# A seventh set of expert weights, and the down weights issued from ScalarE's queue

## What is computed

```python
    flat = g_idx[..., None] * EXPERTS_PER_GROUP + ei              # 4 groups x 8 experts, 2 per token
    combine = jnp.sum(jax.nn.one_hot(flat, N_EXPERTS) * (g_w[..., None] * ew)[..., None], axis=-2)
    a = jnp.einsum('bld,edf->blef', h, w_gate)                    # 32 x 1024 x 256
    u = jnp.einsum('bld,edf->blef', h, w_up)                      # 32 x 1024 x 256
    act = jax.nn.silu(a) * u * combine.astype(h.dtype)[..., None]
    return jnp.einsum('blef,efd->bld', act, w_down)               # 32 x 256 x 1024
...
    y_prompt = rmsnorm(yp, norm_final)
```

## Time and profile before

| | |
|---|---|
| median of three runs | 761.89 us |
| the profiled execution | 762.18 us |
| its span, first to last instruction | 760.4 us |
| moved by the transfers | 243.00 MB, mean 320 GB/s |
| busy: TensorE, VectorE, ScalarE, GpSimd | 655.6, 306.8, 142.4, 139.0 us |

### The profile page before, as it was taken

One profiled execution on the slowest core, in us unless ns is written; L12 is line 12 of the kernel. 1 busy time (PEld: TensorE's weight loads), 2 busy tenths in 40 slices (PEclk: granted clock), 3 DMA queues, 4 the chain that ended last, 5 costly groups with the idle time before them and its releaser, 6 DMA issues.

```text
span 760.4 us, 13782 instructions
## 1 busy us (share of the span) xinstructions
PE 655.6 (86%) x5037; PEld 461.6 (61%) x5037; DVE 306.8 (40%) x1552; ACT 142.4 (19%) x406; POOL 139.0 (18%) x209
## 2 busy tenths in 40 slices
PE   5999999998999978999998999927897879667674
PEld 3888888677888856755432877626653445434331
DVE  3004987998868588610000121354324111111103
ACT  3122223233325322120010000120100101101013
POOL 0169964762000223200000000011000000000000
PEclk9999999999999999999999999957999898899997
DMA  9938989889988988977999989366999999999971
GB/s 309 260 127 281 312 271 401 288 279 342 360 292 281 392 273 287 382 275 275 390 409 386 297 320 409 140 256 239 361 394 401 348 382 401 402 400 402 416 285 59
DMA packets 94918, 243.00 MB, mean 320 GB/s; under 512 B 8850, under 2 KB 54546, under 8 KB 86530
## 3 DMA queue, kind: packets, MB, share of 16 engines
q1 hardware_dynamic: 57906, 192.99, 67.7%
q10 hardware_dynamic: 31328, 32.00, 12.7%
q0 software_dynamic: 5616, 17.11, 6.8%
HBM read 235.00 MB, written 9.11 MB: 321 GB/s over the span
## 4 chain that ended last, share of the span: by engine, by line
PE 56%; DMA 25%; DVE 13%; SPq 2%; issue 2%; ACT 1%; ACTq 0%; POOL 0%; DVEq 0%; POOLq 0%
PE zps L913 32%; DVE kall L1402 6%; PE nps L1087 5%; DMA ring_all<-in_w_up 5%; PE nps L1212 4%; DMA kall<-in_w_up 3%; DMA zret<-in_w_up 3%; DMA gain<-v_rows 3%; DMA qb<-in_w_down 3%; DMA ring_all<-in_w_ret_o 3%; PE zps L1235 3%; DMA out<-sfin 2%; PE nps L884 2%; DMA ring_all<-in_w_down 1%; SPq L444 1%
## 5 line engine op out<-in xcount | busy, mean ns | idle before, releaser
L913 PE MATMUL zps<-hT,ring_all 128*128 128x264 f32 x1152 | 274.8, 393 | 1.6 <-DVE hT L1583 1.0
L913 PEld LDWEIGHTS zps<-hT,ring_all 128*128 128x128 f32 x1152 | 217.4, 193 | 45.0 <-issue 5.3
L1402 DVE CUSTOM_DVE_ANT_0 kall<-kall,qb 128x128 f32<-128x128 f32 x512 | 153.0, 364 | 60.0 <-DMA kall<-in_cache_k 56.9
L620 POOL DMA_INDIRECT zatt<-h_rows,tidx_i x16 | 15.0, 939 | 349.4 <-DVEq L1671 194.4
L913 PE MATMUL zps<-headT,ring_all 128*128 128x264 f32 x256 | 58.5, 388 | 3.7 <-DMA ring_all<-in_w_ret_o 2.3
L913 PEld LDWEIGHTS zps<-headT,ring_all 128*128 128x128 f32 x256 | 48.1, 190 | 14.8 <-issue 4.8
L1087 PE MATMUL nps<-ring_all,zret 128*64 128x512 f32 x224 | 51.6, 599 | 2.8 <-DMA ring_all<-in_cache_v 2.8
L1745 DVE TENSOR_TENSOR qdT<-qdT,nps 128x64 f32<-128x64 f32 x32 | 7.1, 221 | 107.5 <-ACT qdT L825 107.0
L669 ACT ACTIVATE zt<-zps 128x264 f32<-128x264 f32 x56 | 21.8, 390 | 149.4 <-PE zps L913 148.0
L1212 PE MATMUL nps<-ring_all,zatt 128*32 128x128 f32 x768 | 30.0, 311 | 13.9 <-DMA ring_all<-in_w_up 12.4
L1570 DVE TENSOR_TENSOR hT<-zps,zatt 128x264 f32<-128x264 f32 x8 | 3.5, 433 | 93.1 <-PE zps L913 92.9
(11 more groups left out here) (364 smaller groups left out, 839.5 us busy)
## 6 DMA issues: line engine op xcount, KB each, us to landing
kall<-in_cache_k SPq DMA_DIRECT2D x64, 512.0 KB, 6.4
ring_all<-in_cache_v SPq DMA_DIRECT2D x56, 512.0 KB, 8.2
ring_all<-in_w_in ACTq DMA_DIRECT2D x26, 1024.0 KB, 8.8
ring_all<-in_w_gate SPq DMA_DIRECT2D x12, 1024.0 KB, 15.6
ring_all<-in_w_up SPq DMA_DIRECT2D x12, 1024.0 KB, 17.6
ring_all<-in_w_down SPq DMA_DIRECT2D x10, 1024.0 KB, 15.7
ring_all<-in_w_in SPq DMA_DIRECT2D x6, 1024.0 KB, 13.6
kall<-in_w_gate SPq DMA_DIRECT2D x5, 1024.0 KB, 22.8
```

The costliest lines, as they stand in the source:

```text
L620: pool.indirect_dma_start(out=rows, out_offset=None, in_=h2_rows, in_offset=bass.IndirectOffsetOnAxis(ap=col, axis=0), bounds_check=T - 1, ...
L913: mm = pe.matmul(zps[m % 2][:, 0:T], w[:, k, P * fb:P * (fb + 1)], rhs[:, k, :], start=(k == 0), stop=(k == KT - 1))
L1402: ins = v.tensor_tensor_reduce(kh, kh, qb[b % 2][:, P * h:P * (h + 1)], 1.0, 0.0, ALU.mult, ALU.add, scores[:, pg, AH * b + h:AH * b + h + 1])
```

## The change

The number of sets goes from 6 to 7. The seventh's gate and up lie in the first 4,096 columns of `zatt`, its down weights in the columns of the constants that only the mixers use. Small tiles share new ones (`rows_a`, `rows_b`) to make room: `h2n`, `xg`, `xgT` and `ysb` leave `zatt`, for `gain`, `rows_a` and `rows_b`. The two gathered tiles now lie on partitions 0 to 63 and 64 to 127 of `rows_b`; `x_tr` turns them with ordinary matmuls placed in the rows of the array where the data are, not with transposes. `xgT` takes the tile `gain`, so the final gain is loaded by SyncE behind the last expert's gate and up product. The down weights from expert 7 on are issued by ScalarE, a quad's four behind `pick_copy`; SyncE's loop has gate and up alone.

```diff
-SETS = 6
+SETS = 7
...
-        lgs = sb("lgs", [G + NE, T])
+        rows_a, rows_b = sb("rows_a", [P, DM]), sb("rows_b", [P, DM])
...
-        xg = [zflat[0:2 * CAP, DM * i:DM * (i + 1)] for i in range(2)]
-        ysb = zflat[:, 2 * DM:3 * DM]
+        xg = [rows_b[2 * CAP * i:2 * CAP * (i + 1), :] for i in range(2)]
+        ysb = rows_a
...
-        gate_up_w.append(headT[:, :, 0:2048])
+        gate_up_w += [headT[:, :, 0:2048], zflat[:, 0:4096].rearrange("p (a c) -> p a c", a=2)]
...
-                  scr[:, 0:2048], qb_all[:, :, :].rearrange("p a b -> p (a b)")]
+                  scr[:, 0:2048], qb_all[:, :, :].rearrange("p a b -> p (a b)"), cst[:, COL["causal"][0]:COL["causal"][0] + 2048]]
...
-        xgT = [zflat[:, 3 * DM + 512 * i:3 * DM + 512 * (i + 1)] for i in range(2)]
+        xgT = [gain[:, 512 * i:512 * (i + 1)] for i in range(2)]
...
-        h2n = zflat[:, 0:3 * DM].rearrange("p (t d) -> p t d", t=3)
+        h2n = (gain, rows_a, rows_b)
...
             down_in(0, 0)
+            gate_up_in(6, 6)
             sp.wait_ge(z_ready, 2 * (N_IN + 2 * N_O))
             gate_up_in(5, 5)
...
             down_in(1, 1)
+            down_in(6, 6)
...
-            def next_down(e):
-                sp.wait_ge(e_D, 2 * ((e - SETS) // 4 + 1))
-                down_in(e % SETS, e)
-
-            downs = SETS
+
             for e in range(SETS, NE):
                 sp.wait_ge(e_GU, e + 1 - SETS)
                 gate_up_in(e % SETS, e)
-                while downs <= min(e - (4 if e < 16 else 2), NE - 5):
-                    next_down(downs)
-                    downs += 1
...
+            sp.wait_ge(e_GU, NE)
+            sp.dma_start(gain[:, :], norm_final.rearrange("(o d) -> o d", o=1).partition_broadcast(P)
+                         .rearrange("p o d -> p (o d)")).then_inc(fgain, 16)
...
+            for lo, hi in ((0, T), (328, 584), (648, DM)):
+                link(pool.memset(rows_b[:, lo:hi], 0.0))
...
-            act.dma_start(gain[:, :], norm_final.rearrange("(o d) -> o d", o=1).partition_broadcast(P)
-                          .rearrange("p o d -> p (o d)")).then_inc(fgain, 16)
-
...
+            def next_downs(q):
+
+                act.wait_ge(e_D, 2 * (q + 1))
+                for e in range(4 * q + SETS, min(4 * q + SETS + 4, NE)):
+                    if e < NE - 4:
+                        down_in(e)
+                    else:
+                        down_half(e, 0, d_in[e % SETS])
+                if 4 * q + SETS + 4 >= NE:
+                    for e in range(NE - 4, NE):
+                        down_half(e, 1, d_last)
...
                 if e % 4 == 2:
                     pick_copy(e // 4, P, e // 4 + 1)
+                if e % 4 == 2 and e >= 6 and 4 * (e // 4 - 1) + SETS < NE:
+                    next_downs(e // 4 - 1)
...
                 for k in range(KT):
-                    mm = pe.transpose(zps[0][:, 2 * CAP * k:2 * CAP * k + rows], xg[par][0:rows, k:DM:KT], ident[0:rows, 0:rows])
+                    at = slice(2 * CAP * par, 2 * CAP * par + rows)
+                    mm = pe.matmul(zps[0][:, 2 * CAP * k:2 * CAP * k + rows], xg[par][0:rows, k:DM:KT], ident[at, at],
+                                   start=True, stop=True, tile_position=(2 * CAP * par, 0))
```

More of the change, by code:

```diff
@@ L208, in build @@
         zt = [sb(f"zt{i}", [P, T]) for i in range(2)]
+        lgs = zt[0][0:G + NE, :]
         qb_all = sb("qb", [P, 2, DM])
@@ L212, in build @@
         scores = sb("scores", [P, NPG, NB * AH])
-        vnT = sb("vnT", [P, NB * AH])
+        vnT = rows_b[:, 584:584 + NB * AH]
         sn8 = sb("sn8", [NB, AH])
-        rtmp = sb("rtmp", [P, 2, 2, P])
-        rtmd = sb("rtmd", [32 + NB, 1, 2, P])
+        rtmp = rows_a[:, 0:512].rearrange("p (a b c) -> p a b c", a=2, b=2)
+        rtmd = rows_b[0:32 + NB, 328:584].rearrange("p (a b c) -> p a b c", a=1, b=2)
         scr = sb("scr", [P, 2304])
@@ L224, in build @@
         qdT = sb("qdT", [P, P])
-        s1 = sb("s1", [P, RDV])
-        sfin = sb("sfin", [P, RDV])
-        qkd = sb("qkd", [P, 2, RH * NB])
+        s1, sfin = rows_a[:, 512:768], rows_a[:, 768:1024]
+        qkd = rows_b[:, 264:328].rearrange("p (a b) -> p a b", a=2)
         ptab = sb("ptab", [1, NB * NPG], I32)
@@ L350, in build @@
             "y_square", "t_oh", "t_pos", "t_lhs", "t_idx", "t_e2"))
-        t_x, t_exp, t_tabs = map(sem, (
-            "t_x", "t_exp", "t_tabs"))
+        t_exp, t_tabs = map(sem, (
+            "t_exp", "t_tabs"))
         x_in2 = [sem(f"xg_in{i}") for i in range(2)]
@@ L362, in build @@
         fgain = sem("fgain")
-        h2_scaled = sem("h2_scaled")
         block = ctx.enter_context(nc.Block())
@@ L484, in _ @@
                 gate_up_in(e % SETS, e)
-                while downs <= min(e - (4 if e < 16 else 2), NE - 5):
-                    next_down(downs)
-                    downs += 1
[L488 to L492, removed]
-                    sp.dma_start(down_w[e % SETS].rearrange("p (f n) -> p f n", f=FB)[:, :, 512 * half:512 * (half + 1)],
-                                 w_down[0, bass.ds(e, 1), :, 512 * half:512 * (half + 1)].rearrange("o (f p) n -> p (o f) n", p=P)
-                                 ).then_inc(signals[e % SETS] if signals else d_last, 16)
             sp.wait_ge(t_exp, 1)
@@ L622, in gather @@
                                         bounds_check=T - 1, oob_is_err=False).then_inc(x_in2[par], 16)
-            def gather_for(p):
+            for p in range(NPAIR):
                 if p >= 2:
@@ L627, in gather_for @@
                 gather(p % 2, xg[p % 2], tidx_i[0:2 * CAP, p:p + 1])
-            for p in range(2):
-                gather_for(p)
-            for p in range(2, NPAIR):
-                gather_for(p)
             base = link_n[0]
@@ L794, in _ @@
                 copy(xT[:, k, :], zps[k % 2][:, 0:T]).then_inc(x_Tc, 1)
+            act.wait_ge(r_st, 16 * RH)
             act.wait_ge(v_used, N_V)
@@ L835, in y_copy, with down_in, down_half @@
                 copy(ysb[rows, 512 * half:512 * (half + 1)], bank[rows, :]).then_inc(e_Dc, 1)
+            def down_in(e):
+                act.dma_start(down_w[e % SETS].rearrange("p (f n) -> p f n", f=FB),
+                              w_down[0, bass.ds(e, 1)].rearrange("o (f p) n -> p (o f) n", p=P)).then_inc(d_in[e % SETS], 16)
+            def down_half(e, half, signal):
+                act.dma_start(down_w[e % SETS].rearrange("p (f n) -> p f n", f=FB)[:, :, 512 * half:512 * (half + 1)],
+                              w_down[0, bass.ds(e, 1), :, 512 * half:512 * (half + 1)].rearrange("o (f p) n -> p (o f) n", p=P)
+                              ).then_inc(signal, 16)
+            def next_downs(q):
[8 more added lines that the diff above has]
+                        down_half(e, 1, d_last)
             def pick_copy(q, rows, n):
@@ L1182, in tile_base @@
             def tile_base():
-                pe.wait_ge(t_x, 1)
+                pe.wait_ge(t_lhs, 3)
                 pe.matmul(mps[:, 640:640 + NE], xcnt_b, upper[0:NE, 0:NE], start=True, stop=True)
@@ L1187, in tile_rows @@
             def tile_rows():
-                pe.wait_ge(t_lhs, 3)
+                pe.wait_ge(t_lhs, 4)
                 row_table(bps[:, 768:768 + XT], xA, xB)
@@ L1694, in tile_counts @@
                 link(v.tensor_copy(xcnt_b, xcnt.to_broadcast([NE, P])))
-                v.sem_inc(t_x, 1)
+                v.sem_inc(t_lhs, 1)
             def tile_tables():
```

8 lines of the change are left out of this document (4 added, 4 removed).

## The result

The changed kernel takes 780.07 us in the median of four runs (777.95 to 781.06), against 761.5 us for the kernel before beside it: a ratio of 1.023, with a 95% interval of 1.0197 to 1.0264. I had forecast 757.0 us, faster by a little. It is slower by 15 to 20 us by the interval, 18.6 us by the medians. The profiled execution took 779.74 us, its span is 777.9 us.

The account below looks back on a forecast made before the run. Weight transfers, not TensorE, were taken to bound the expert stage. Terms -8.0 - 1.5 + 1.2 + 2.4 + 1.0 = -4.9 us took the median of 761.89 to 757.0 us, range 751 to 765.

Parts of the forecast that it names:

- The 15 other pairs: Matmul turns after the first in the expert stage: 0.6 us more each, hidden in TensorE's slack, so 0.
- The first pair's term (+2.4): First turn behind the router, at half clock: matmuls dearer than transposes and delaying SyncE's next transfer, +2.4 us.
- the first rival: At the turn and the final gain: the turn is no dearer and the gain hides, 753.6 us; chance 0.22.
- The tail: Last experts' weights: the last halves, issued by ScalarE behind `pick_copy`, start later and leave the DMA engines idle, +1.2 us.
- The two terms of ScalarE's queue, -1.5 and +1.2: Moving down weights: -1.5 us for DMA dips at 549 and 606 us removed, +1.2 us for last halves issued later.
- The seventh set's -8.0: Around the router: three transfers leave the saturated expert stage for idle DMA time, -8.0 us.
- the gain's +1.0: Final gain's 512 KB load, moved into the tail beside the last halves, +1.0 us.
- The fourth rival: Expert stage: two queues of weights lower the transfer rate, up to 18 us more, 775 us; chance 0.13.
- the figure of the sum: Expert stage: 396 GB/s as the rate of the full DMA engines, making a 1,024 KB transfer worth 2.65 us.
- The third: Rival at the router: the seventh down transfer delays the first gather by up to 2.65 us, 759.7 us; chance 0.08.
- The fill: Seventh set's early transfers around the router: gate and up fill 475 to 480 us, down weights end about 509.1.
- The second rival: ScalarE's issues block in the expert stage, 2.77 us each, 11 us a quad, giving 760 us; chance 0.12.

Follow-up runs that it names:

- e1: The changed kernel with the gathered rows turned by transposes again, ScalarE's queue and seven sets kept: 761.41 us, ratio 0.9976.
- e3: The changed kernel with each turning matmul loading 128 neighbouring columns instead of every eighth: 766.04 us, ratio 1.0044.
- e8: The changed kernel with the turning matmuls loading every second column instead of every eighth: 766.8 us in its one run.
- e9: The changed kernel with turning matmuls for pairs 0 to 7 only and transposes for 8 to 15: 769.78 us, ratio 1.0103.
- e4: The changed kernel with transposes again and the down weights back in SyncE's queue, seven sets kept: 757.03 us, ratio 0.9894.
- e12: Repeat of e4 (seven sets, transposes, SyncE's queue alone) on another chip: 756.53 us, ratio 0.9946.
- e5: The kernel before with down weights from expert 6 on issued by ScalarE; six sets, transposes, early gain: 767.57 us, ratio 1.0028.
- e6: e1 with each gate and each up transfer cut in two of 4 KB rows: 762.41 us, ratio 0.9976.
- e2: The kernel before with the turn by ordinary matmuls, all on partitions 0 to 63: 790.69 us, ratio 1.0295.

## Why the prediction was wrong

**The step that failed** is "The 15 other pairs add 0.6 us each, 9 us in all, beside 48 us of slack: 0." Each adds 2.9 us, 44 us in all, of 48, and it was not hidden: e1, without them and the first, is 18.7 us faster. The first pair's term (+2.4) was nearly right: measured 2.9 us, and SyncE's first issue stands 519.19 - 510.59 = 8.6 us behind the start of the turn where it stood 5.7 us behind. What was wrong was the row for full clock. I took 0.105 us from line 1122, a matmul whose weights are neighbouring columns; the turn loads every eighth. At half clock my nearest row had the right number for another reason: there the clock sets the pace, and the step hardly shows (0.23 to 0.25 us). At full clock the step does. The rows had a hint: the transposes took 1.11 and 1.09 us at either clock. I read it, in the first rival, as a sign that the turn might be cheap. It said that something other than the array's clock set their pace. For the matmuls e3 and e8 show what: the step; for the transposes no run varies it. For a form with twice the instructions at that step I had no row, and should have kept 4 us as the upper bound for every turn.

The sentence from the Trainium skill that I set beside it ("TensorE: Matmul & The Clock Gate", section "Terms", the transpose mode four times as fast for float32) is nearly what the trace shows for this turn: 4.03 against 1.11 us, 3.6 times. I worked it out for the first pair only. For all sixteen, as an estimate from that page, it would have been 3.3 x 16 = 53 us, over the slack. At a step of 1 the runs don't show it: 2.00 us against the transposes' 1.09 us at a step of 8, and transposes at a step of 1 were not run.

**Slack is not one sum.** Even 9 us would probably not have been free, as e3 suggests. Only 5.5 of the 48 us of idle time lay in 520 to 560 us, where TensorE decides when sets come free; in that stretch of the kernel before it is busy for 34.52 of 40 us:

```profile
520.00:560.00 40.00, 34.52 (x687) 25.75 (x688) 15.29 (x64) 5.77 (x22) 3.73 (x4) 0.95 0.97 363
```

There e9 lost 10 us. The rest lay behind it, where TensorE waited for weights. A use of slack has to be priced where it stands.

**The tail** was the second term mis-sized. The two terms of ScalarE's queue, -1.5 and +1.2, made -0.3 us; e1 against e4 and e12 makes it +4 to +5. The +1.2 priced only that the last halves are issued later (728.15 for 726.99 us), with "a low share for some 4 us". That a batch of down weights beside gate and up takes 25 to 38 us to land, and TensorE waits for it, stands nowhere in it: "ScalarE's queue has had 31 us to empty its last four" was used for the length of an issue alone. In e1 expert 27's down weights are issued at 707.35 and landed at some 723 us, and the engines are idle for 9.0 us. Its two dips did go, as the -1.5 had it.

**What held.** The seventh set's -8.0 with the gain's +1.0, -7.0 us, stands against e4 and e12 (-8.1 and -4.1 us by their ratios), and the stage moves 2.5 transfers less. The dips at 549 and 606 us are gone in e1 (share 1.00 in 520 to 560, 1.02 in 560 to 640). The fourth rival, a lower rate with two queues, is not seen: 396 GB/s at a share of 1.02 in the kernel after, in 640 to 680 us, the figure of the sum; over 560 to 700 us it is 389 with two queues (e1) and 391 with one (e4), both a little under it. The third is not either: TensorE waits 5.17 us for the first gather and waited 5.18 us. The fill took its hole, in part in the profiled execution after (0.39 in 475 to 480 us for 0.02), wholly in e4_sync_downs (1.01); in e1 it is 0.87. The stretch of 505 to 510 has 0.13 for 0.28 in the kernel after, but only because its router is done 3.7 us earlier: the same stretch before the first turn, now 501.3 to 506.3, has 0.76. So the seventh down transfer went where it was meant to. The final gain was issued at 752.89, behind ScalarE's last half as supposed. The second rival happened, but seldom. In ScalarE's queue of e1_transpose an issue takes half a us or less, but for the fourth of a quad, which is blocked once for 6.43 us and once for 1.93:

```profile
605.68 0.37 ACTq L822 DMA_DIRECT2D ring_all<-in_w_down  x1
...
607.12 6.43 ACTq L822 DMA_DIRECT2D scr<-in_w_down  x1
...
674.92 1.93 ACTq L822 DMA_DIRECT2D qb<-in_w_down  x1
```

Left open: the exact price of ScalarE's queue (the intervals of e1, e4 and e12 touch), whether it costs anything with six sets (e5 says 3 us, within the scatter), and what holds the clock down where the dear turns stand.

## What to carry to other kernels

Price a changed form of instruction from a row with the same access pattern, the step of its operands included, and at both clocks; where a row runs at one pace at either clock, something other than the array's clock sets it. Cost that is put down to slack has to be put against the slack of its own stretch. And an order in one queue is also a priority: when two kinds of transfer get queues of their own, ask which kind now lands early without use, and what the engine has left to do when the other kind arrives.

## What the runs showed of the hardware

- A float32 matmul instruction with weights of 64 partitions x 128 columns and 64 moving columns, at full clock: 0.125 us with neighbouring weight columns (2.00 / 16), 0.131 with every second (2.10 / 16), 0.25 with every eighth (4.01 / 16). At half clock 0.23, 0.23, 0.25 us. The float32 transpose of the same every-eighth columns is one instruction of 0.14 us at both (1.11 / 8 and 1.09 / 8).
- A queue with 4 KB rows beside a saturated one with 8 KB rows landed 1 MB transfers, issued four at a time, in 25 to 38 us; beside one with 4 KB rows, in transfers of half the size, in 15 to 22 us (medians by tile, e1 and e6).
- In 520 to 560 us the granted clock is 0.63 to 0.71 in the three kernels whose turns there are matmuls with every eighth column (e2, after, e9), with TensorE busy for 38 of the 40 us, and 0.82 to 0.95 in the eleven others, with TensorE busy for 33 to 37 us.
